# Two down projections of a two-block network: seven block products in place of eight

## The reference, cut to what matters

```python
# first block
x = x + g2 * _conv_ffn(h2, w_up[l], conv_w[l], conv_b[l], w_down[l])
...
# second block: conv_ffn ends in
return (jax.nn.gelu(a, approximate=False) * g) @ w_down
```

## Time and profile before

| what | value |
|---|---|
| runs (3) | median 2507.37 us, 2505.81 to 2509.82 |
| the profiled execution, its own time | 2507.51 us |
| its span, first to last instruction | 2505.7 us |
| granted TensorE clock, mean | 0.988 of full |
| busy PE / DVE / ACT / POOL | 95% / 65% / 41% / 22% |
| first down projection | 904.9 to 1138.5 us of the span |
| second down projection | 2249.0 to 2487.5 us |

### The profile page before, as it was taken

The page is one execution under the profiler, slowest core; times in us unless marked ns, Lnnn a source line. Parts: engine busy times, 40 slices in busy tenths (PEclk is TensorE's granted clock), DMA queues, the critical chain, the costliest instruction groups (busy, mean ns, idle before and its releaser), DMA issues. The chain is left out here.

```text
span 2505.7 us, 38163 instructions
## 1 busy us (share of the span) xinstructions
PE 2390.1 (95%) x16353; PEld 1291.5 (52%) x16353; DVE 1634.7 (65%) x2158; ACT 1019.3 (41%) x1219; POOL 561.4 (22%) x296
## 2 busy tenths in 40 slices
PE   7989889999999999999999999988989999999997
PEld 3447664444444444444767776774434444444443
DVE  6788847565545554555477878786878877773343
ACT  5117417345454531323354545442344444441221
POOL 0010000057777711000000000000036766630000
PEclk9999999999999999999999999999999999999998
DMA  9117674121212144443200000003112121225342
GB/s 338 34 53 237 195 229 160 62 73 52 67 51 68 51 148 122 110 109 127 64 26 18 26 26 23 21 26 126 51 51 67 51 68 51 68 64 176 94 114 90
DMA packets 307687, 224.62 MB, mean 90 GB/s; under 512 B 11424, under 2 KB 298302, under 8 KB 306367
## 3 DMA queue, kind: packets, MB, share of 16 engines
q1 hardware_dynamic: 306646, 221.86, 29.3%
q10 hardware_dynamic: 873, 0.32, 0.1%
HBM read 199.61 MB, written 22.03 MB: 88 GB/s over the span
## 5 line engine op out<-in xcount | busy, mean ns | idle before, releaser
L200 PE MATMUL ps<-hT,arena 128*128 128x512 bf16 (+1 forms) x2592 | 552.4, 374 | 15.8 <-DVE arena L2185 5.9
L2118 PE MATMUL ps<-hT,arena 128*128 128x512 bf16 x2280 | 498.9, 379 | 0.3 <-DVE ps L2269 0.3
L1923 PE MATMUL ps<-arena 128*128 128x512 bf16 x2106 | 459.0, 380 | 2.5 <-DVE arena L1907 2.5
L200 PEld LDWEIGHTS ps<-hT,arena 128*128 128x128 bf16 x2592 | 252.7, 98 | 313.3 <-issue 20.3
L2118 PEld LDWEIGHTS ps<-hT,arena 128*128 128x128 bf16 x2280 | 223.0, 98 | 269.8 <-issue 1.3
L1923 PEld LDWEIGHTS ps<-arena 128*128 128x128 bf16 x2106 | 206.3, 98 | 251.8 <-DVE arena L1907 3.8
L2194 POOL TENSOR_TENSOR arena<-arena 128x2048 f32<-128x2048 f32 x2 | 12.6, 6282 | 1138.7 <-DVE arena L696 1138.7
L2407 DVE SCALAR_TENSOR_TENSOR xT<-ps,vec,xT 128x945 f32<-128x945 f32 (+2 forms) x176 | 215.1, 1222 | 31.9 <-ACT xT L2390 26.4
L1907 DVE TENSOR_TENSOR arena<-hT,arena 128x2816 bf16<-128x2816 f32 x30 | 92.8, 3093 | 181.8 <-ACT arena L1902 181.6
L2118 PE MATMUL ps<-xT,arena 128*128 128x512 bf16 x912 | 203.0, 379 | 0.0
L2185 POOL TENSOR_TENSOR arena<-arena 128x2048 bf16<-128x2048 f32 x38 | 156.4, 4115 | 100.6 <-ACT arena L2177 100.6
(11 more groups left out here) (454 smaller groups left out, 3291.8 us busy)
## 6 DMA issues: line engine op xcount, KB each, us to landing
xT<-ada_w_dram SPq DMA_DIRECT2D x24, 1024.0 KB, 5.9
arena<-w_up_dram SPq DMA_DIRECT2D x44, 512.0 KB, 5.1
arena<-ffn_up_dram SPq DMA_DIRECT2D x44, 512.0 KB, 5.2
hT<-w_down_dram SPq DMA_DIRECT2D x30, 704.0 KB, 7.6
hT<-ffn_down_dram SPq DMA_DIRECT2D x30, 704.0 KB, 7.0
arena<-w_in_dram SPq DMA_DIRECT2D x33, 512.0 KB, 4.1
xT<-w_mod_dram SPq DMA_DIRECT2D x16, 1024.0 KB, 6.2
arena<-w_mod_dram SPq DMA_DIRECT2D x8, 1024.0 KB, 19.4
```

The source lines that it names most:

```text
L200: last = pe.matmul(out, lhs(a, kt), rhs(b, kt, i), start=start and kt == 0 and (a, b) == (0, 0), stop=stop and kt == n_k - 1 and (a, b) == ...
L1923: last = pe.matmul(self.bank(u), self.part(u, a, kt), self.g[:, b, kt, cols], start=kt == 0 and (a, b) == (0, 0), stop=kt == FT - 1 and (a ...
L2118: last = pe.matmul(out, self.stationary(u, block, a, kt), moving(b, kt), start=start and kt == 0 and (a, b) == (0, 0), stop=kt == 3 and (a ...
```

## The change

The down projection Y = W g is cut in two by output features, by rows of W (11 tiles each) and by tokens, and computed by the seven products of the Winograd form of Strassen's method. There are 28 jobs, 7 products x 4 output tiles, each of 11 x 3 = 33 matmuls of 128x512 (`JOBS`). Products 2, 3 and 4 go on in the bank of product 1, 6 and 7. Each bank is added to x as soon as it is read: to three, two or one of the four quarters (`TARGETS`), 44 updates in place of 16. The weights come as halves, 36 loads of 704 KB in place of 32. POOL forms the 16 sums of weight blocks (128x1408 each) and the low parts of the last six jobs. The combinations of the gated values are formed in place: the first, row by row, by POOL during the up projection; the second by one POOL subtraction of 128x5632; the third by DVE in 44 steps of 256 elements; the fourth by POOL in 22 steps of 512. Five operands of 128x5632 are split by ACT and DVE. The gate's multiplication is two instructions of 512, and the splits of the gated values cover 512 elements instead of 1024. The norms beside the projection move to its last six jobs, the norm of half 0 in part behind it, and in the last stage half 1 is transposed and averaged behind the last job. POOL's masks come behind its down work.

```diff
...
+            row = u - HALF_K
+            if row >= 0:
+                pool.wait_ge(self.done, row + 1)
+                pool.wait_ge(self.combined, 4 + 2 * row)
+                for part in range(2):
+                    value = self.g_first[:, row, :].rearrange("p (h n) -> p h n", h=2)
+                    if part:
+                        pool.wait_ge(self.combined, 4 + 2 * row + 1)
+                    pool.tensor_tensor(value, value, self.b11[:, row, :, part, :], ALU.subtract).then_inc(self.combined, 1)
...
-        c = self.conv_of(u, 0)
-        dve.tensor_tensor(c, c, self.conv_of(u, 1), ALU.mult).then_inc(self.multiplied, 1)
+        c, gate = self.conv_of(u, 0), self.conv_of(u, 1)
+        dve.tensor_tensor(self.second_half(u), self.second_half(u), gate[:, HALF:T], ALU.mult)
+        dve.tensor_tensor(self.g_first[:, u, :], c[:, 0:HALF], gate[:, 0:HALF], ALU.mult).then_inc(self.multiplied, 1)
...
+class DownProducts:
...
+    JOBS = [(1, 0), (1, 1), (1, 2), (1, 3), (2, 0), (2, 1), (2, 2), (5, 0), (2, 3), (6, 0), (5, 1), (3, 0), (6, 1), (5, 2),
+            (3, 1), (6, 2), (5, 3), (3, 2), (6, 3), (7, 0), (3, 3), (7, 1), (7, 2), (7, 3), (4, 0), (4, 1), (4, 2), (4, 3)]
+    TARGETS = {1: (12, 21, 22), 2: (11,), 5: (12, 22), 6: (21, 22), 3: (12,), 7: (22,), 4: (21,)}
+    CHAINED = {2: 1, 3: 6, 4: 7}
...
+    SUMS = [("S1", 0), ("S2", 0), ("S1", 1), ("S4", 0), ("S2", 1), ("S1", 2), ("S4", 1), ("S2", 2), ("S1", 3), ("S4", 2),
+            ("S2", 3), ("S3", 0), ("S4", 3), ("S3", 1), ("S3", 2), ("S3", 3)]
+    SUM_OF = {5: "S1", 6: "S2", 3: "S4", 7: "S3"}
...
+    FOURTHS_BEHIND = {("S4", 0): 2, ("S2", 1): 3, ("S2", 2): 3, ("S4", 2): 3}
+    POOL_FROM = 22
...
+        sp.wait_ge(f.a_lo, FT)
+        bring(sp, "F", 1, 1, 0, (1, 0))
+        sp.wait_ge(f.s_lo, FT - f.PLAIN)
+        bring(sp, "R3", 1, 1, 1, (1, 1))
+        sp.wait_ge(f.multiplied_out, f.product_count(FT - 1, 6))
+        self.residual(sp, slice(0, 4))
+        sp.wait_ge(f.done, FT - 1)
+        self.residual(sp, slice(4, 6))
+        sp.wait_ge(f.made, f.made_count(FT - 1))
+        bring(sp, "R0", 1, 1, 2, (1, 2))
+        bring(sp, "R1", 1, 1, 3, (1, 3))
+        split(1, 0)
+        bring(sp, "R2", 1, 2, 0, (2, 0))
+        split(1, 1)
+        bring(sp, "R3", 1, 2, 1, (2, 1))
+        sp.wait_ge(f.done, FT)
+        self.residual(sp, slice(6, KD))
...
+    def pe(self, pe, hook=lambda i, kt: None):
+        f = self.f
+        operand_ready = {5: 5, 3: 6, 6: 7, 7: 8, 4: 9}
+        for i, (product, n) in enumerate(self.JOBS):
+            pe.wait_ge(self.lo, i + 1)
+            if (product, n) == (1, 0):
+                pe.wait_ge(f.done, FT - 1)
+            if (product, n) == (2, 0):
+                pe.wait_ge(f.done, FT)
+            if product in operand_ready and n == 0:
+                pe.wait_ge(f.t_lo, operand_ready[product])
+            if product in self.CHAINED:
+                pe.wait_ge(self.read, self.updates_until(self.job(self.CHAINED[product], n)))
+            elif product == 7:
+                pe.wait_ge(self.read, self.updates_until(self.job(2, n)))
+            elif product in (5, 6) and n >= 2:
+                pe.wait_ge(self.read, self.updates_until(self.job(5 if product == 5 else 3, n - 2)))
+            for kt in range(HALF_K):
+                hook(i, kt)
+                for a, b in PASSES:
+                    last = pe.matmul(self.bank(i), self.w[:, i % 2, a, kt, :], self.moving(product, b, kt),
+                                     start=product not in self.CHAINED and kt == 0 and (a, b) == (0, 0),
+                                     stop=kt == HALF_K - 1 and (a, b) == PASSES[-1], skip_group_check=True)
+            last.then_inc(self.made, 1)
...
+    def split_hi(self, act, i):
+        product, n = self.JOBS[i]
+        if i >= 2:
+            act.wait_ge(self.made, i - 1)
+        else:
+            act.wait_ge(self.f.made, self.f.made_count(FT - 2))
+        if product in self.SUM_OF:
+            act.wait_ge(self.f.summed, self.sum_count(self.SUM_OF[product], n))
+        else:
+            slot, count = self.needed[(product, n)]
+            act.wait_ge(self.loaded[slot], count)
+        act.activation(self.w[:, i % 2, 0], self.raw[self.place(i)], ACT.Copy).then_inc(self.hi, 1)
+
+    def split_lo(self, eng, i):
+        eng.wait_ge(self.hi, i + 1)
+        eng.tensor_tensor(self.w[:, i % 2, 1], self.raw[self.place(i)], self.w[:, i % 2, 0], ALU.subtract).then_inc(self.lo, 1)
...
+    def third_combination(self, dve, rows):
+
+        f = self.f
+        dve.wait_ge(f.combined, self.T2_DONE)
+        dve.wait_ge(self.made, self.job(1, 3) + 1)
+        for r in rows:
+            for h in range(2):
+                last = r == HALF_K - 1 and h == 1
+                f.link(dve.tensor_tensor(self.spare_half, self.b11[:, r, h, 0, :], self.b11[:, r, h, 1, :], ALU.add))
+                done = dve.tensor_tensor(self.t3_f32[:, r, h, :], self.x[:, r, h * HALF // 2:(h + 1) * HALF // 2], self.spare_half,
+                                         ALU.subtract)
+                if last:
+                    done.then_inc(f.apart_set, 1)
+                else:
+                    f.link(done)
...
+    def update(self, dve, i):
+        product, n = self.JOBS[i]
+        dve.wait_ge(self.made, i + 1)
+        if i == 0:
+            dve.wait_ge(self.x_home, 48)
+        for target in self.TARGETS[product]:
+            row, column = divmod(target, 10)
+            t = 4 * (row - 1) + n
+            x = self.k.xT[:, t, 0:HALF] if column == 2 else self.k.xT[:, t, HALF:T]
+            if (t, column) in self.updated:
+                dve.wait_ge(self.read, self.updated[(t, column)])
+            self.read_count += 1
+            self.updated[(t, column)] = self.read_count
+            dve.scalar_tensor_tensor(x, self.bank(i), self.gate(t), x, ALU.mult, ALU.add).then_inc(self.read, 1)
...
+    def act(self, act, also=lambda i: None):
+        for i in range(2, len(self.JOBS)):
+            if i + 1 < len(self.JOBS):
+                self.split_hi(act, i + 1)
+            for step, product in ((2, 5), (3, 3), (5, 6), (17, 7), (20, 4)):
+                if i == step:
+                    self.operand_hi(act, product)
+            also(i)
+
+    def dve(self, dve, also=lambda i: None):
+        self.read_count, self.updated = 0, {}
+        for i in range(2, len(self.JOBS)):
+            if i + 1 < min(self.POOL_FROM, len(self.JOBS)):
+                self.split_lo(dve, i + 1)
+            if i == 2:
+                self.update(dve, 0)
+            self.update(dve, i - 1)
+            for step, product in ((2, 5), (4, 3), (6, 6), (18, 7), (21, 4)):
+                if i == step:
+                    self.operand_lo(dve, product)
+            if 9 <= i < 15:
+                self.third_combination(dve, range(2 * (i - 9), min(2 * (i - 9) + 2, HALF_K)))
+            also(i)
+        self.update(dve, len(self.JOBS) - 1)
...
+    def pool(self, pool):
+        f = self.f
+        pool.wait_ge(f.t_lo, 5)
+        pool.wait_ge(f.multiplied, FT)
+        pool.tensor_tensor(self.x, self.y, self.x, ALU.subtract).then_inc(f.combined, 1)
+        count, row = self.T2_DONE, 0
...
+            pool.tensor_tensor(self.raw[out], self.raw[a], self.raw[b], op).then_inc(f.summed, 1)
+            for _ in range(self.FOURTHS_BEHIND.get((name, n), 0)):
+                if row == 0:
+                    pool.wait_ge(self.made, self.job(2, 3) + 1)
+                hi, lo = (self.b21[:, row, s, :] for s in range(2))
+                pool.wait_ge(f.combined, count)
+                pool.tensor_tensor(self.spare, hi, lo, ALU.add).then_inc(f.combined, 1)
+                pool.wait_ge(f.combined, count + 1)
+                pool.tensor_tensor(self.t4_f32[:, row, :], self.spare, self.x[:, row, :], ALU.subtract).then_inc(f.combined, 1)
+                count, row = count + 2, row + 1
+            for i in range(self.POOL_FROM, len(self.JOBS)):
+                if (name, n) == ("S3", 3):
+                    self.split_lo(pool, i)
...
+            f.sync(sp, down, context)
+            sp.wait_ge(down.lo, down.job(4, 1) + 1)
+            short.load(sp, 2)
+            sp.wait_ge(c_norm.ready, KD)
+            sp.dma_start(ctx_dram, k.hT[:, :, :, 0:CTX]).then_inc(ctx_saved, 16)
+            short.load(sp, 3)
             sp.wait_ge(ctx_saved, 16)
             short.load(sp, 0)
-            sp.wait_ge(down.made, last_u)
+            sp.wait_ge(down.made, last_job)
             short.load(sp, 1)
-            sp.wait_ge(down.made, 2 * KD)
-            for n in range(2, len(parts)):
-                short.load(sp, n)
+            sp.wait_ge(down.made, len(down.JOBS))
...
+            down.dve(dve, beside)
+            total(1, 7)
+            m_norm.dve_finish(dve, (0,))
+            short.lo(dve, 0)
+            short.lo(dve, 1)
...
+            down.pool(pool)
...
+            def row_block(t):
+                if t >= 1:
```

(53 more changed lines are left out.)

521 lines of the change are left out of this document (274 added, 247 removed).

## The result

The kernel after the change takes **2577.70 us** (median of 4 runs, 2574.82 to 2585.56) beside 2506.59 for the kernel before: ratio 1.0288, 95% interval 1.0261 to 1.0314. The forecast was 2592, slower, and its sign and its main cause held. The profiled run spans 2573.9 us, 68.2 more than before.

A forecast was written before the change was run, and what follows sets the result against it. PE was taken to bound both down projections, with room on its helpers. Terms -57.0 - 2.5 + 10.4 + 110 + 14 + 5 + 5 = +85 on 2507.37 gave 2592 us; own range 2560 to 2625, wider range 2528 to 2640.

The forecast's parts named there:

- PE: Down projections: 924 matmuls instead of 1056 each, -57.0 us in all; before's idle time goes too, -2.5.
- Up projections: POOL's added operations make sums slip about 1 us per period, but PE's matmuls cover it: 0.
- Opening, job 4: Job 4's low part waits on DVE behind late x, updates and operand split: +5.2 us per projection, +10.4.
- Port, jobs 5 to 22: POOL's and DVE's two-SBUF-input instructions take turns, stalling PE: 55 us taken per projection, +110.
- walk: Stepping the 28 jobs through by predicted durations, each engine in its own order: 60 us of stalls.
- The clock falls too: Rival, chance 0.07: PE's holes also lower its clock, some 44 us more than the forecast's stalls, 2640 and above.
- End of the first projection: Short convolution waits for DVE's last update, total, half 0's norm and a weight split: 14.1 us, +14.
- The norm beside jobs 24 to 27: Norm work packed beside the first projection's last jobs adds between 0 and 9 us: +5.
- Moved work: Context loads, transposes, norm and POOL's masks, moved later, stay covered: 0, up to 5 us if cover is gone.
- End of the second: From last update to mean: a row's finish and four reductions, 7.2 us where before took 2.4: +5.
- slack hides the port: Rival, chance 0.07: lo split waits stay below 4.1 us, no stalls arise, seven products pay: -25, 2482 us.
- Weights come too late: Rival, chance 0.08: 36 loads per projection, sent in fixed order behind waits, arrive late: about 20 more, 2610 us.

The follow-up runs named there:

- e10: Kernel after the change, with job 22's low part made by DVE instead of POOL and operand 7's two parts one job earlier: 2569.34 us.
- e1: Kernel after the change, with the second combination's one POOL subtraction of 128x5632 made as 11 of 128x512: 2570.41 us.
- e2: Kernel after the change, with the fourth combination's 22 POOL additions replaced by memsets of about the same length that read no SBUF: 2552.20 us.
- e4: Kernel after the change, with the fourth combination (22 POOL additions of 512 elements per projection) left out altogether: 2551.53 us.
- e5: Kernel after the change, with all of POOL's down projection work moved to DVE at hand-placed steps and operands placed anew: 2499.84 us.
- e6: Kernel after the change, with extra unread matmuls filling PE's waits ahead of jobs 5, 11 and 14: 2577.81 us.

## Why the prediction was right, point by point

- ***PE*, -57.0 and -2.5**: 1848 matmuls, as said. Right in number and pitch.
- ***Up projections*, 0**: the first down matmul comes 0.8 us later, the way from the short convolution to the second projection is 4.0 us shorter. Near enough: with the same instructions up to there, the first down matmul came at 902.3 us in e10 and at 905.9 in e1.
- ***Opening, job 4*, +10.4**: mis-sized. It was 0.97 and 1.91. The last quarter of x was on hand for the first update at +18.1 us, not at +22; the updates (4.04), the operand split (6.01) and the low part (1.62) behind it took what was said.
- ***Port, jobs 5 to 22*, +110**: the cause held in most of the signs that were named. DVE's low parts averaged 2.4 and 4.1 us beside a shortest of 1.6, the long subtraction (13.4) had a DVE split end 1.5 behind it, and e2 against e4 shows that the reading of SBUF is what costs. Of the walk's places jobs 5 (6.1 for 6.7), 22 (5.3 for 5.6) and 11 (9.4 for 13) came near; job 14 had 5.9 and 10.4 for 13; job 6 had 0.3 for 3.7. The idle time came to 82.6 us for the 110 taken, the slower matmuls to 27.3. Together that is 109.9, or 50.8 and 59.1 by projection. That it meets the 110 so closely is luck: 55 was picked between a bound of 28.5 and a walk of 60, and the single places were off both ways (jobs 7 and 13 had 1.9 and 2.1 us where the walk had none). Not all of it is POOL's doing: e5 takes 82 us out of the two stretches and still has some 20 us of holes in front of jobs 5 to 22, from DVE's own list. Two signs came otherwise. PE's busy time fell by 34 us and not by 57, because matmuls at the lower clock last longer. POOL was busy 139.5 and 127.2 us for 110, as it waits for the port too (its sums took 3.5 to 5.9 us on average by form, and 3.15 at their shortest).
- ***The clock falls too*, costed at 0 in the sum**: right, though the clock fell as the earlier trace rows had shown. The prediction's reason, that the port catches up while PE runs slowly, is what e6 shows: without the slow matmuls PE idles longer and the stretches stay 261 us long. The 82.6 and the 27.3 us are one loss in two forms, and the helpers' pace set it.
- ***End of the first projection*, +14**: 15.8. The last update began 2.2 us behind the last matmul, as the update of job 26 and two totals still stood ahead of it on DVE, which the step left out. The norm beside jobs 24 to 27, +5, was 1.9.
- ***Moved work*, 0**: held; the load of the first short unit landed 4.2 us after its issue, ahead of ACT's need.
- ***End of the second*, +5**: 4.7.

The sum was 14 us too high beside the medians, 17 beside the 68.2 of the profiled runs: the opening (7.5), the norm beside the last jobs (3.1), the 4.0 us that the part between the projections gave back, and about 3 us of half 1's transposes, which no longer stand inside the second stretch, less the 1.8 at the first end and 0.8 ahead of it. Two small sums in the prediction don't come out (6.3, 8.7 and 1.1 are 16.1 and not 17; the last pieces are 7.0 and not 7.2); neither changes a term. The rival *slack hides the port* (2482) fell for this kernel, but e5 shows its place: with the mean hole in front of jobs 5 to 22 at 0.6 us, below the 0.7 that it named, the seven products pay, by 0.3%. *Weights come too late* had no sign in front of PE: of the 87.4 us of idle time none was released by a transfer. That is a weak sign, as PE waits for split weights and never for a load. One step further back loads are late. POOL waited 60 and 72 us for them in the two stretches, also ahead of job 22:

```profile
1100.53 3.15 POOL L2645 TENSOR_TENSOR arena<-arena 128x1408 f32<-128x1408 f32 x1 [7.61 <-DMA arena<-w_down_dram]
1103.64 11.88 POOL L2521 TENSOR_TENSOR arena<-arena 128x1408 bf16<-128x1408 f32 x2
```

In e5 the same loads feed sums on DVE, which stood idle 0.2 us in front of all of them together. No run moved the loads alone, so their share in after's holes stays open.

## What to carry to other kernels

Price work that is moved to POOL by what it takes from DVE, not by how empty POOL is: here each of POOL's two-input instructions lasted about twice as long as the same one on DVE and kept DVE's two-input ones out meanwhile, so that DVE did the whole in less of its own time. When PE idles in front of a helper's instruction, look at the shortest time of that form beside its mean, before moving anything in the order: mending single gaps (e1, e10) or the clock (e6) gave 0 to 8 us, moving POOL's work to DVE gave 78. And cutting a long instruction only moves the wait if the engine that holds the port is on the path itself.

## What the runs showed of the hardware

- POOL's memset of 1400 elements (1.26 us) ran beside DVE's two-input steps without changing their 0.42 us (e2).
- One DVE instruction of 1.6 us showed as 11.52: the profile counts waiting for the port as busy time, so DVE's 215 us in the first projection held less work than the 201 of e5.
- Eleven chained POOL pieces of 1.27 us let three DVE instructions in between, which took 0.3 to 1.1 us more than undisturbed (e1): the turns alternate even when one engine has its next instruction ready.
- Behind holes of 5.9 to 10.4 us the next 33 matmuls lasted 9.0 to 10.3 us in place of 7.3, and filling a hole with other matmuls brought 7.3 back (e6).
